# Stores of the expert blocks' result rows issued from ScalarE's queue in place of GpSimd's

## The chip, the cores and the metric

The kernel runs on one core of a Trainium2 chip. The metric is the device time of one execution in microseconds (us), from the start of the program to its end; lower is better. All values are float32.

## The reference

One inference step of a hybrid encoder layer for 336 rows (tokens) of width 1024: 64 sample rows, 16 meta rows and 256 prompt rows. Two branches (an mLSTM memory and a latent attention) are mixed and added to the rows; then every row goes to 4 of 32 experts, and a last RMSNorm follows. The change touches only the expert part:

```python
logits = x2 @ w_router + b_router
top_v, top_i = top_k(logits, 4); gates = softmax(top_v)
# rows sorted by expert, each expert's rows padded to whole blocks -> xs
def expert_block(xb, e):
    gu = xb @ w_gu[e] + b_gu[e]                    # 1024 -> 2048
    gate = minimum(gu[:, :1024], 7); up = clip(gu[:, 1024:], -7, 7)
    hid = (up + 1) * gate * sigmoid(1.702 * gate)
    return hid @ w_dn[e] + b_dn[e]                 # 1024 -> 1024
out = zeros.at[token].add(ys[dest] * gate)
```

The kernel adds the bias `b_dn` elsewhere (as gates times `b_down`), so that a block's result row is only `hid @ w_dn[e]`.

## The kernel before

Every engine has its own instruction stream, written out by hand, and the streams meet at counting semaphores. Before the expert part come the norms, the input projection, both branches and the router (to about 743 us of the span). DVE then works out, from the router's choice, how many blocks of 64 rows there are (`nb`, 39 for these inputs), which expert each block belongs to (`bei`), and which row of the sorted copy each token takes (`desti`). GpSimd (POOL) scatters the rows into a DRAM buffer `x_rows`, sorted by expert.

**The loop over blocks.** All five engines run a loop over these 39 blocks. Some experts have two blocks. An expert's weights are 12 pieces of 1 MB, each in one fixed place of the buffer `ring`: `up_w(0..7)` (gate and up weights, 8 KB in each of 128 partitions) and `dn_w(0..3)` (down weights). There is one place for each piece, so SyncE (SP) can issue the load of a piece for the next expert only when TensorE (PE) has read the piece in the current expert's last block. SP issues the loads in the order of PE's reading: `up_w(6)` and `up_w(7)` after PE's line 886, then `dn_w(0..3)` during line 906, then `up_w(0..5)` during line 878 (lines 521 and 525 are SP's).

In a block PE does, in this order: gate and up products for k = 0 to 5 (line 878), then k = 6 and 7 (line 886), transposes of the next block's rows out of `xrow` (line 546), the bias of the next block (line 867), transposes of `hid`, and the down product (line 906) into PSUM bank 4, whose halves of 64 partitions hold the two halves of the 1024 result columns. DVE clamps and multiplies (lines 1184, 1187, 1190).

ScalarE (ACT) does in each block: the sigmoid (line 1143), the copy of the turned tokens (to `xg`), the copy of the turned hidden values (`hidT`, semaphore `m_hidT`), and the copy of the result from bank 4 into `yrow`, which lies in the buffer `r_xt` (line 1149; the profile shows copies under the helper's line 933, as `r_xt<-bank`). `yrow` is a single buffer of 128 partitions by 512 columns.

POOL does in each block: the load of the next but one block's rows into `xrow` (line 1612, shown as `r_v<-x_rows`, 256 KB), the two stores of `yrow` to the DRAM buffer `y_rows` (line 1616, 64 rows of 2 KB each, 128 KB each), then it waits until the stores have landed (`m_store`) and raises `yrow_free`. PE waits for `yrow_free` before the next block's down product. After the loop POOL gathers the result rows of each token from `y_rows` (12 indirect transfers, line 1626), DVE weighs and adds them, and the last norm and the output stores follow.

In the profile's names, SPq, ACTq and POOLq are the instruction queues of those engines, and FUSED_REGOPS and MOVE there are register work for a transfer's address.

Of the kernel before, what the change touches and what calls it, by code (L numbers as in the profile page):

```python
# [33 lines left out]
NE, TOPK, BLK = 32, 4, 64  # L34
# [137 lines left out]
def build(nc, i, o, x_rows_dram, y_rows_dram):  # L172
    with ExitStack() as ctx:
# [3 lines left out]
        def sem(name):  # L177
            return ctx.enter_context(nc.semaphore(name))
# [133 lines left out]
        yrow = r_xt[:, 1280:1792]  # L312

        def up_w(k):
            at = UPSLOT[k // 2] * SLOT + 2 * D * (k % 2)
            return ring[:, at:at + 2 * D]

        def dn_w(j):
            at = DNSLOT[j // 2] * SLOT + 2 * D * (j % 2)
            return ring[:, at:at + 2 * D].rearrange("p (h f) -> p h f", h=2)  # L320
# [40 lines left out]
             "m_dve", "m_pick", "m_turn", "m_hidT", "fin_v", "fin_ss", "fin_s", "fin_out", "all_out"))  # L361
        m_rows_in, m_read = sem("m_rows_in"), sem("m_read")
        desti_set, blocks_out, x_sent = sem("desti_set"), sem("blocks_out"), sem("x_sent")
        yrow_free, zero_set, rows_zeroed = sem("yrow_free"), sem("zero_set"), sem("rows_zeroed")
        fin_y = [sem(f"fin_y{t}") for t in range(3)]
        dve_step, act_step = sem("dve_step"), sem("act_step")

# [162 lines left out]
        def _(pe):  # L530
            def begin(*name):
                n = JOB[name]
                if n >= 8:
                    pe.wait_ge(bank_free[n % 8], n // 8)
                return banks[n % 8]
# [9 lines left out]
            def turn(out, src):  # L545
                return pe.transpose(out, src, ident[0:src.shape[0], 0:src.shape[0]])  # L546
# [3 lines left out]
            b = begin("vecT")  # L550
            end(turn(b[:, 0:NVEC], vec_rows[0:NVEC, :]), "vecT")
            b = begin("convT")
            end(turn(b[:, 0:48], conv_rows[:, :]), "convT")

            for t, (c0, n) in enumerate(ROWS):
                pe.wait_ge(xn_ready, t + 1)
                for s in range(2):
                    b = begin("xT", t, s)
# [23 lines left out]
            for t in range(4):  # L582
                b = begin("cacheT", t)
# [3 lines left out]
            for name, lo, hi in (("ssq", 0, 3), ("ssk", 3, 5)):  # L587
                pe.wait_ge(cq_ready, hi)
                b = begin(name)
                end(group(b[:, 0:NT], [(cst("ones"), sq[:, k, :]) for k in range(lo, hi)]), name)  # L590
            taken(pe, "kr")
            b = begin("krs")
# [15 lines left out]
            for t, (c0, m) in enumerate(KEYS):  # L608
                b = begin("kvrow", t)
# [4 lines left out]
            b = begin("cols")  # L614
# [11 lines left out]
            for hp in range(4):  # L626
                b = begin("ukT", hp)
# [12 lines left out]
                for h in (0, 1):  # L640
                    taken(pe, "qr", hp, h)
                    b = begin("qrs", hp, h)
# [4 lines left out]
                for n in range(4):  # L647
                    h, r = n // 2, n % 2
                    b = begin("ql", hp, n)
# [56 lines left out]
                for h in (0, 1):  # L706
                    b = begin("ov", hp, h)
# [5 lines left out]
            for h in range(4):  # L713
                b = begin("wi", h)
                end(group(b[:, 0:NT], [(cst("sel", 4)[:, 128 * h:128 * h + 128], R_WI)]), "wi", h)
            for h in range(4):
                b = begin("mx", h)
                end(group(b[0:64, 0:NT], [(cst("sel", 4)[:, 128 * h:128 * h + 64], R_MX)]), "mx", h)
            pe.wait_ge(tail_done, 16)
            b = begin("convrow")  # L720
# [17 lines left out]
            for c, (c0, m) in enumerate(CHUNKS):  # L738
                q0 = qcol(c0)
                for s in range(2):  # L740
                    b = begin("krow", c, s)
# [3 lines left out]
                for s in range(2):  # L745
                    b = begin("vrow", c, s)
# [3 lines left out]
                b = begin("s", c)  # L750
# [17 lines left out]
                for h in range(4):  # L768
                    b = begin("num", c, h)
# [6 lines left out]
                for n in range(8):  # L776
                    b = begin("upd", c, n)
# [4 lines left out]
                if c in (0, 5):  # L782
                    for n in range(8):
                        taken(pe, "upd", c, n)
                    b = begin("nT", c)
# [15 lines left out]
            for t, (c0, m) in enumerate(ROWS):  # L801
                for s in range(2):
                    panel_here(pe, f"wo{s}")
                    b = begin("out", t, s)
                    end(group(b[0:m, :], [(mixed[:, k, c0:c0 + m], PV[f"wo{s}"][:, k, :]) for k in range(8)]),
                        "out", t, s)
            for t, (c0, m) in enumerate(ROWS):
                pe.wait_ge(x2_ready, t + 1)
                for s in range(2):
                    b = begin("x2T", t, s)  # L810
# [4 lines left out]
            for t, (c0, m) in enumerate(ROWS):  # L815
                for s in range(2):
                    taken(pe, "x2T", t, s)
                b = begin("lg", t)
# [3 lines left out]
            for t, (c0, m) in enumerate(ROWS):  # L822
                b = begin("pos", t)
# [3 lines left out]
            b = begin("cnt")  # L827
# [3 lines left out]
            for t, (c0, m) in enumerate(ROWS):  # L831
                pe.wait_ge(gates_set, t + 1)
                b = begin("gT", t)
                end(turn(b[0:NE, 0:m], gmat[0:m, t, :]), "gT", t)
            for t, (c0, m) in enumerate(ROWS):
                taken(pe, "gT", t)
                for s in range(2):
                    b = begin("bd", t, s)
# [5 lines left out]
            def tokens_turned():  # L844

                for k in range(8):
                    ins = turn(xt_bank[:, BLK * k:BLK * k + BLK], xrow[:, 128 * k:128 * k + 128])
                ins.then_inc(m_gath, 1)
# [7 lines left out]
            nb = pe.value_load(nbi[0:1, 0:1].bitcast(I32), min_val=NE, max_val=MAXB)  # L856
# [3 lines left out]
            def half(bank, t):  # L860
                return bank[BLK * t:BLK * t + BLK, :]

            def bias(b):

                pe.wait_ge(m_pick, b + 1)
                for q in range(4):
                    pe.matmul(half(gate_bank if q < 2 else up_bank, q % 2), pick[:, q, :], bgu[:, :],  # L867
                              start=True, stop=False, skip_group_check=True)

            bias(0)  # L870
            with pe.Fori(0, nb) as b:
                e = pe.value_load(bei[0:1, bass.ds(b, 1)].bitcast(I32), min_val=0, max_val=NE - 1)
                pe.wait_ge(m_xg, b + 1)
                for k in range(6):
                    pe.wait_ge(up_in[k], 16 * e + 16)
                    w = up_w(k)
                    for q in range(4):
                        ins = pe.matmul(half(gate_bank if q < 2 else up_bank, q % 2), xg[:, k, :],  # L878
                                        w[:, 512 * q:512 * q + 512], start=False, stop=False, skip_group_check=True)
                    ins.then_inc(m_up, 1)  # L880
                for k in (6, 7):
                    pe.wait_ge(up_in[k], 16 * e + 16)
                for bank_, q0, done in ((gate_bank, 0, m_gate), (up_bank, 2, m_up)):
                    for k in (6, 7):
                        for t in range(2):
                            ins = pe.matmul(half(bank_, t), xg[:, k, :],  # L886
                                            up_w(k)[:, 512 * (q0 + t):512 * (q0 + t) + 512], start=False,
                                            stop=(k == 7), skip_group_check=True)
                    ins.then_inc(done, 1)
                pe.wait_ge(m_xrow, 16 * b + 32)  # L890
                pe.sem_inc(m_rows_in, 1)
                tokens_turned()
                pe.wait_ge(m_read, b + 1)
                bias(b + 1)
                pe.wait_ge(m_hid, b + 1)
                for j in range(4):
                    ins = turn(ht_bank[:, 128 * j:128 * j + 128], hid[:, 128 * j:128 * j + 128])
                ins.then_inc(m_turn, 1)
                pe.wait_ge(m_hidT, b + 1)
                pe.wait_ge(yrow_free, b + 1)  # L900
                for j in range(4):
                    pe.wait_ge(dn_in[j], 16 * e + 16)
                    w = dn_w(j)
                    for h in range(2):
                        for t in range(2):
                            ins = pe.matmul(half(out_bank, t), hidT[:, j, BLK * h:BLK * h + BLK],  # L906
                                            w[:, h, 512 * t:512 * t + 512], start=(j == 0 and h == 0),
                                            stop=(j == 3 and h == 1), skip_group_check=True)
                    ins.then_inc(m_down, 1)
# [3 lines left out]
        def _(act):  # L913
# [14 lines left out]
            def signal(ins, s, v):  # L928
                ins.then_inc(s, 1)
                act.wait_ge(s, v)  # L930

            def copy(out, src, scale=1.0):
                return act.activation(out, src, ACT.Copy, scale=scale)  # L933
# [141 lines left out]
            for c, (c0, m) in enumerate(CHUNKS):  # L1075
# [7 lines left out]
                for s in range(2):  # L1083
                    filled(act, "krow", c, s)
                    p = bank(("krow", c, s))
                    h = 2 * s
# [48 lines left out]
            nb = act.value_load(nbi[0:1, 0:1].bitcast(I32), min_val=NE, max_val=MAXB)  # L1135
            def tokens():
                return copy(xg[:, :, :], banks[0][:, :].rearrange("p (k s) -> p k s", k=8))

            act.wait_ge(m_gath, 1)
            signal(tokens(), m_xg, 1)  # L1140
            with act.Fori(0, nb) as b:
                act.wait_ge(m_gt, b + 1)
                act.activation(sg, gt, ACT.Sigmoid, scale=ALPHA).then_inc(m_sig, 1)  # L1143
                act.wait_ge(m_gath, b + 2)
                tokens().then_inc(m_xg, 1)
                act.wait_ge(m_turn, b + 1)
                copy(hidT[:, :, :], banks[1][:, :].rearrange("p (j s) -> p j s", j=4)).then_inc(m_hidT, 1)
                act.wait_ge(m_down, 4 * b + 4)
                copy(yrow, banks[4][:, :]).then_inc(m_yrow, 1)
                act.wait_ge(m_yrow, b + 1)  # L1150
                act.wait_ge(moe_tab, 1)
                act.nop()


            for t, (_, n) in enumerate(ROWS):
# [392 lines left out]
        def _(pool):  # L1548
# [52 lines left out]
            pool.dma_start(xrow, x_rows_dram[0:BLK, :]).then_inc(m_xrow, 16)  # L1601
            pool.wait_ge(moe_tab, 1)
            nb = pool.value_load(nbi[0:1, 0:1].bitcast(I32), min_val=NE, max_val=MAXB)
            pool.sem_inc(yrow_free, 1)
            pool.wait_ge(m_gath, 1)
            pool.dma_start(xrow, x_rows_dram[BLK:2 * BLK, :]).then_inc(m_xrow, 16)
            with pool.Fori(0, nb) as b:
                src = x_rows_dram[bass.ds(pool.snap(b * BLK + 2 * BLK), BLK), :]
                dst = y_rows_dram[bass.ds(pool.snap(b * BLK), BLK), :]
                pool.wait_ge(m_gath, b + 2)  # L1610
                pool.wait_ge(moe_tab, 1)
                pool.dma_start(xrow, src).then_inc(m_xrow, 16)  # L1612
                pool.wait_ge(m_yrow, b + 1)
                pool.wait_ge(moe_tab, 1)
                for h in range(2):
                    pool.dma_start(dst[:, 512 * h:512 * h + 512], yrow[BLK * h:BLK * h + BLK, :]).then_inc(m_store, 16)  # L1616
                pool.wait_ge(m_store, 32 * b + 32)
                pool.sem_inc(yrow_free, 1)
            pool.wait_ge(m_store, 32 * nb)
            pool.wait_ge(m_xrow, 16 * nb + 32)  # L1620
            word = u_pad[0:1, 0, 67:68]
            pool.tensor_tensor(word, word, word, ALU.add).then_inc(blocks_out, 1)
# [50 lines left out]
```

## Time and profile before

| | |
|---|---|
| time, median of 3 runs | 1902.02 us (1899.36 to 1903.99) |
| the profiled execution | 1902.52 us |
| its span, first to last instruction | 1900.9 us |
| mean granted TensorE clock over the span | 0.948 of full |
| PE busy | 1640.6 us (86%) |
| DVE, ACT, POOL busy | 373.1, 372.1, 116.3 us |
| moved by the 16 DMA engines | 511.29 MB, mean 269 GB/s |
| expert loop | about 743 to 1854 us of the span |

"Busy" counts no register, wait or DMA-issuing work of SP and ACT. POOL's transfers do count as POOL's busy time. "To landing" is the time from the issue of a transfer to the semaphore that says its last byte is there. The span leaves out some 1.6 us of the execution's time.

### The profile page before, as it was taken

Reading aid. Unit: us, or ns where it says so; the run is one execution under the profiler, and the core shown is the slowest. Engines: PE = TensorE matmul, PEld = TensorE weight load, DVE = VectorE, ACT = ScalarE, POOL = GpSimd, SP = SyncE. Lnnn points to the kernel's source line nnn. Section 1 sums busy time; section 2 is a strip of 40 time slices with the busy share of each in tenths; the row PEclk is TensorE's granted clock in tenths of the full one; section 3 lists DMA queues with packets and bytes.
Section 4 is the critical chain, followed back from the end, with each engine's and each line's share of the span. In section 5 each row is a group of like instructions: output and inputs, shape, how many; then the busy total and the mean of one; then the engine's idle time right before and its main releaser. Section 6 shows DMA issues by size and latency. Waiting matters only on the chain.

```text
span 1900.9 us, 20283 instructions
## 1 busy us (share of the span) xinstructions
PE 1640.6 (86%) x7096; PEld 742.0 (39%) x7097; DVE 373.1 (20%) x899; ACT 372.1 (20%) x722; POOL 116.3 (6%) x220
## 2 busy tenths in 40 slices
PE   2999999999999986978788998877899978898890
PEld 1556656566666542322223332222233322232330
DVE  1444442223231134110101110101011101110114
ACT  1333432254430020111111111111111101111111
POOL 0010000000000002000000000000000000000003
PEclk9989899899999976999999999999999999999995
DMA  9355442111207425999997999999898999589884
GB/s 292 122 141 131 120 118 89 67 68 45 89 22 272 184 89 194 401 401 408 407 403 305 383 351 403 401 410 400 336 401 327 399 410 401 219 317 400 332 353 149
DMA packets 115540, 511.29 MB, mean 269 GB/s; under 512 B 11601, under 2 KB 15422, under 8 KB 82606
## 3 DMA queue, kind: packets, MB, share of 16 engines
q1 hardware_dynamic: 98862, 454.98, 61.1%
q0 software_dynamic: 16640, 55.81, 10.2%
q8 instruction: 22, 0.36, 0.1%
q14 instruction: 16, 0.13, 0.0%
HBM read 471.21 MB, written 39.55 MB: 269 GB/s over the span
## 4 chain that ended last, share of the span: by engine, by line
PE 58%; DMA 32%; DVE 4%; issue 2%; SPq 2%; ACT 1%; POOL 1%; DVEq 0%; POOLq 0%; ACTq 0%
DMA ring<-in_w_gate_up 31%; PE bank L542 31%; PE bank L878 9%; PE bank L886 8%; PE bank L906 6%; PE bank L546 2%; PE bank L867 2%; DMA ring<-in_w_in 1%; DVE r_c L1190 1%; POOL x_rows L1597 1%; DVE r_kv L1184 1%; SPq L521 1%; ACT r_kv L933 1%; SPq L433 0%; DVE r_qk L1190 0%
## 5 line engine op out<-in xcount | busy, mean ns | idle before, releaser
L878 PE MATMUL bank<-ring,r_kv 128*64 128x512 f32 x1872 | 422.4, 596 | 38.8 <-DMA ring<-in_w_gate_up 38.6
L906 PE MATMUL bank<-ring,r_kv 128*64 128x512 f32 x1248 | 276.4, 595 | 26.8 <-ACT r_kv L933 26.8
L542 PE MATMUL bank<-r_xt,ring 128*128 128x336 f32 (+2 forms) x896 | 273.7, 462 | 5.8 <-DMA ring<-in_w_in 5.4
L878 PEld LDWEIGHTS bank<-ring,r_kv 128*64 128x64 f32 x1872 | 128.5, 137 | 326.5 <-issue 226.0
L1184 DVE TENSOR_SCALAR r_kv<-bank 128x512 f32<-128x512 f32 (+1 forms) x80 | 55.0, 687 | 993.9 <-PE bank L886 981.1
L886 PE MATMUL bank<-ring,r_kv 128*64 128x512 f32 x624 | 160.3, 660 | 56.9 <-DMA ring<-in_w_gate_up 56.9
L542 PEld LDWEIGHTS bank<-r_xt,ring 128*128 128x128 f32 (+2 forms) x896 | 167.5, 190 | 98.6 <-issue 26.3
L906 PEld LDWEIGHTS bank<-ring,r_kv 128*64 128x64 f32 x1248 | 86.0, 137 | 192.1 <-issue 156.0
L1143 ACT ACTIVATE r_o<-r_kv 128x512 f32<-128x512 f32 x39 | 24.6, 630 | 544.0 <-DVE r_kv L1184 544.0
L886 PEld LDWEIGHTS bank<-ring,r_kv 128*64 128x64 f32 x624 | 51.9, 152 | 162.5 <-issue 162.5
L542 PE MATMUL bank<-ring 128*128 128x336 f32 (+4 forms) x336 | 96.4, 429 | 4.1 <-DVE ring L1343 3.9
L867 PE MATMUL bank<-bgu,r_qk 128*64 128x512 f32 x320 | 78.9, 614 | 8.8 <-DVE r_kv L1184 8.8
L933 ACT ACTIVATE r_kv<-bank 128x512 f32<-128x512 f32 (+3 forms) x85 | 49.9, 587 | 162.1 <-PE bank L546 161.8
L933 ACT ACTIVATE r_xt<-bank 128x512 f32<-128x512 f32 x39 | 23.3, 598 | 280.3 <-PE bank L906 280.3
L542 PE MATMUL bank<-ring,r_kv 128*128 128x128 f32 (+6 forms) x256 | 72.7, 421 | 2.1 <-DVE r_kv L1187 1.2
L542 PEld LDWEIGHTS bank<-ring 128*128 128x128 f32 (+4 forms) x336 | 58.1, 181 | 38.8 <-issue 15.7
L546 PEld LDWEIGHTS bank<-const,r_v 64*128 64x128 f32 (+3 forms) x524 | 45.1, 138 | 67.5 <-issue 31.9
L1616 POOL DMA_DIRECT2D y_rows<-r_xt x78 | 41.9, 537 | 414.0 <-ACT r_xt L933 411.9
L546 PE MATMUL bank<-const,r_v 64*128 64x64 f32 (+3 forms) x524 | 61.4, 253 | 1.8 <-DMA r_v<-x_rows 1.8
L542 PE MATMUL bank<-r_kv,ring 128*128 128x336 f32 (+10 forms) x240 | 60.9, 386 | 0.0
L1612 POOL DMA_DIRECT2D r_v<-x_rows x39 | 20.6, 529 | 632.9 <-PE bank L546 600.5
L542 PEld LDWEIGHTS bank<-ring,r_kv 128*128 128x128 f32 (+4 forms) x256 | 40.9, 192 | 35.7 <-issue 26.8
(213 smaller groups left out, 1001.9 us busy)
## 6 DMA issues: line engine op xcount, KB each, us to landing
ring<-in_w_gate_up SPq DMA_DIRECT2D x256, 1024.0 KB, 20.3
ring<-in_w_down SPq DMA_DIRECT2D x128, 1024.0 KB, 22.7
ring<-in_w_in SPq DMA_DIRECT2D x12, 2048.0 KB, 9.1
r_v<-x_rows POOLq DMA_DIRECT2D x41, 256.0 KB, 7.4
y_rows<-r_xt POOLq DMA_DIRECT2D x78, 128.0 KB, 5.5
x_rows<-r_c POOLq DMA_DIRECT2D x7, 1024.0 KB, 6.9
x_rows<-r_c POOLq DMA_DIRECT2D x9, 768.0 KB, 5.7
y_rows<-r_c POOLq DMA_DIRECT2D x1, 5376.0 KB, 31.1
```

What stands on the lines that cost most here:

```text
L521: sp.dma_start(up_w(k), gu[:, bass.ds(e, 1), k, :].rearrange("p a f -> p (a f)")).then_inc(up_in[k], 16)
L542: ins = pe.matmul(out, l, r, start=(n == 0), stop=(n == len(pairs) - 1), **kw)
L546: return pe.transpose(out, src, ident[0:src.shape[0], 0:src.shape[0]])
L867: pe.matmul(half(gate_bank if q < 2 else up_bank, q % 2), pick[:, q, :], bgu[:, :], start=True, stop=False, skip_group_check=True)
L878: ins = pe.matmul(half(gate_bank if q < 2 else up_bank, q % 2), xg[:, k, :], w[:, 512 * q:512 * q + 512], start=False, stop=False, skip_gr ...
L886: ins = pe.matmul(half(bank_, t), xg[:, k, :], up_w(k)[:, 512 * (q0 + t):512 * (q0 + t) + 512], start=False, stop=(k == 7), skip_group_che ...
L906: ins = pe.matmul(half(out_bank, t), hidT[:, j, BLK * h:BLK * h + BLK], w[:, h, 512 * t:512 * t + 512], start=(j == 0 and h == 0), stop=(j ...
L933: return act.activation(out, src, ACT.Copy, scale=scale)
L1143: act.activation(sg, gt, ACT.Sigmoid, scale=ALPHA).then_inc(m_sig, 1)
L1184: return dve.tensor_scalar(out, a, s1, s2, op0, op1)
L1612: pool.dma_start(xrow, src).then_inc(m_xrow, 16)
L1616: pool.dma_start(dst[:, 512 * h:512 * h + 512], yrow[BLK * h:BLK * h + BLK, :]).then_inc(m_store, 16)
```

## The change

The two stores leave POOL's loop and are issued by ACT right behind the copy that fills `yrow`. `yrow_free` goes. PE's down product now waits for the copy of the block before (`m_yrow`), which is what frees bank 4. ACT waits for the landing of the block before's stores (`m_store`) before it overwrites `yrow`. POOL keeps the loads of `xrow`, and waits for all stores once, behind its loop.

```diff
@@ PE, down product
-                pe.wait_ge(yrow_free, b + 1)
+                pe.wait_ge(m_yrow, b + 1)
@@ ACT, loop over blocks
+            act.sem_inc(m_store, 1)
+            act.sem_inc(m_yrow, 1)
             with act.Fori(0, nb) as b:
+                dst = y_rows_dram[bass.ds(act.snap(b * BLK), BLK), :]
...
                 act.wait_ge(m_down, 4 * b + 4)
+                act.wait_ge(m_store, 32 * b + 1)
                 copy(yrow, banks[4][:, :]).then_inc(m_yrow, 1)
-                act.wait_ge(m_yrow, b + 1)
+                act.wait_ge(m_yrow, b + 2)
                 act.wait_ge(moe_tab, 1)
-                act.nop()
+                for h in range(2):
+                    act.dma_start(dst[:, 512 * h:512 * h + 512], yrow[BLK * h:BLK * h + BLK, :]).then_inc(m_store, 16)
@@ POOL, loop over blocks
-            pool.sem_inc(yrow_free, 1)
...
-                dst = y_rows_dram[bass.ds(pool.snap(b * BLK), BLK), :]
                 pool.wait_ge(m_gath, b + 2)
                 pool.wait_ge(moe_tab, 1)
                 pool.dma_start(xrow, src).then_inc(m_xrow, 16)
-                pool.wait_ge(m_yrow, b + 1)
-                pool.wait_ge(moe_tab, 1)
-                for h in range(2):
-                    pool.dma_start(dst[:, 512 * h:512 * h + 512], yrow[BLK * h:BLK * h + BLK, :]).then_inc(m_store, 16)
-                pool.wait_ge(m_store, 32 * b + 32)
-                pool.sem_inc(yrow_free, 1)
-            pool.wait_ge(m_store, 32 * nb)
+            pool.wait_ge(m_store, 32 * nb + 1)
             pool.wait_ge(m_xrow, 16 * nb + 32)
```

ACT's queue before, from the table load ahead of the sigmoid to the branch back at the loop's end (`r_xt` is `yrow`'s buffer, ISA and REGISTER_ALU are register work):

```order
L1143 ACT_TABLE_LOAD
L1143 ACTIVATE r_o<-r_kv 128x512 [waits m_gt]
L1144 REGISTER_ALU
L933 ACTIVATE r_kv<-bank 128x512 [waits m_gath]
L933 ACTIVATE r_kv<-bank 128x512 [waits m_turn]
L1148 ISA
L933 ACTIVATE r_xt<-bank 128x512 [waits m_down]
L1141 REGISTER_ALU [waits moe_tab,m_yrow]
L1141 COMPARE_AND_BRANCH
```

The same place of ACT's queue in the changed kernel:

```order
L1146 ACT_TABLE_LOAD
L1146 ACTIVATE r_o<-r_kv 128x512 [waits m_gt]
L1147 REGISTER_ALU
L933 ACTIVATE r_kv<-bank 128x512 [waits m_gath]
L933 ACTIVATE r_kv<-bank 128x512 [waits m_turn]
L1151 ISA
L1152 ISA [waits m_down]
L933 ACTIVATE r_xt<-bank 128x512 [waits m_store]
L1157 ISA [waits moe_tab,m_yrow]
L1157 DMA y_rows<-r_xt 64x512
L1157 ISA
L1157 DMA y_rows<-r_xt 64x512
```

The copy now has a wait of its own for the landing of the stores before, and two DMA issues stand between it and the branch, behind which the next block's table load and sigmoid come.

POOL's queue before, from the loop's one load to the gather behind the loop:

```order
L1612 DMA r_v<-x_rows 64x1024
L1613 REGISTER_ALU
L1616 ISA [waits moe_tab,m_yrow]
L1616 DMA y_rows<-r_xt 64x512
L1616 ISA
L1616 DMA y_rows<-r_xt 64x512
L1617 ISA
L1607 REGISTER_ALU [waits m_store]
L1607 COMPARE_AND_BRANCH
L1619 REGISTER_ALU
L1620 ISA [waits m_store]
L1622 TENSOR_TENSOR u_pad<-u_pad 1x1 [waits m_xrow]
```

The same place in the changed kernel:

```order
L1615 DMA r_v<-x_rows 64x1024
L1611 REGISTER_ALU
L1611 COMPARE_AND_BRANCH
L1616 ISA
L1617 ISA [waits m_store]
L1619 ISA
L1619 TENSOR_TENSOR u_pad<-u_pad 1x1 [waits m_xrow]
```

In the last block the wait for the landing now comes behind the loop, so the loop's own closing instructions no longer follow that landing.

## Rows read from the trace of the kernel before

**Rows 1.** The page: the chain that ended last, shares of the span.

```profile
DMA ring<-in_w_gate_up 31%; PE bank L542 31%; PE bank L878 9%; PE bank L886 8%; PE bank L906 6%; PE bank L546 2%; PE bank L867 2%; DMA ring<-in_w_in 1%; DVE r_c L1190 1%; POOL x_rows L1597 1%; DVE r_kv L1184 1%; SPq L521 1%; ACT r_kv L933 1%; SPq L433 0%; DVE r_qk L1190 0%
```

**Rows 2.** Chain in order of time, expert loop: start us, us, what.

```profile
814.54 27.84 DMA ring<-in_w_gate_up
...
945.34 26.64 DMA ring<-in_w_gate_up
...
1734.94 27.85 DMA ring<-in_w_gate_up
```

**Rows 3.** DMA queues in 797 to 1004 us.

```profile
DMA packets 15410, 84.01 MB, mean 406 GB/s; under 512 B 1552, under 2 KB 1552, under 8 KB 8759
q1 hardware_dynamic: 14258, 80.60, 96.9%
```

**Rows 4.** Line 1616, the stores, over the whole execution.

```profile
L1616 POOL DMA_DIRECT2D y_rows<-r_xt x78: 529/540/544, 774.6 to 1854.8; - x78
DMA to landing us min/median/max: 2.3/5.5/6.4
```

**Rows 5.** Waits in 744 to 1900 us: waited for, us, times, longest us.

```profile
ACT r_o L1143 <- DVE r_kv L1184: 544.0, 39, 19.7
PE bank L906 <- ACT r_kv L933: 26.8, 39, 0.7
```

**Rows 6.** Timeline of ACT: a block of one expert, and the last block.

```profile
923.90 0.60 ACT L933 ACTIVATE r_xt<-bank 128x512 f32<-128x512 f32 x1 [7.19 <-PE bank L906]
924.83 1.28 ACT L1143 ACT_TABLE_LOAD   x1 [0.33 <-ACT r_xt L933]
943.70 0.63 ACT L1143 ACTIVATE r_o<-r_kv 128x512 f32<-128x512 f32 x1 [17.59 <-DVE r_kv L1184]
...
1840.74 0.63 ACT L1143 ACTIVATE r_o<-r_kv 128x512 f32<-128x512 f32 x1 [10.95 <-DVE r_kv L1184]
```

**Rows 7.** SP's issues, whole execution (ns min/median/max), and two stretches from 916 us.

```profile
L521 SPq DMA_DIRECT2D ring<-in_w_gate_up x248: 332/346/3298, 750.2 to 1817.1; - x124
L525 SPq DMA_DIRECT2D ring<-in_w_down x1: 8387/8387/8387, 924.0 to 924.0; - x1
L521 SPq DMA_DIRECT2D ring<-in_w_gate_up x1: 2823/2823/2823, 933.8 to 933.8; - x1
L521 SPq DMA_DIRECT2D ring<-in_w_gate_up x3: 877/1011/1038, 939.2 to 941.7; - x3
```

**Rows 8.** Timeline of PE, 944 to 978 us: where a block waits for its weights.

```profile
961.66 1.94 PE L878 MATMUL bank<-ring,r_kv 128*64 128x512 f32 x8 [0.70 <-DMA ring<-in_w_gate_up]
...
972.12 5.35 PE L886 MATMUL bank<-ring,r_kv 128*64 128x512 f32 x16 [3.15 <-DMA ring<-in_w_gate_up]
```

**Rows 9.** DMA queue of POOL in 924 to 934 us, one block's two stores.

```profile
q0 software_dynamic: 96, 0.26, 6.6%
```

**Rows 10.** DMA queue of SP in 365 to 373 us, one load in 2 KB rows.

```profile
q1 hardware_dynamic: 1040, 2.10, 73.5%
```

**Rows 11.** The same in 414 to 422 us.

```profile
q1 hardware_dynamic: 1024, 2.07, 68.4%
```

**Rows 12.** Chain in order of time, from the last block's copy to the gather.

```profile
1852.90 0.61 ACT r_xt L933
...
1854.76 2.49 DMA y_rows<-r_xt
...
1857.79 0.20 POOL u_pad L1622
...
1862.40 6.12 DMA ring<-y_rows,r_qk
```

**Rows 13.** Line 521, over the whole execution: the weight loads' landing.

```profile
DMA to landing us min/median/max: 4.9/20.4/28.0
```


**Rows 14.** DMA issues in 0 to 40 us: the smallest row load on SP's queue.

```profile
ring<-in_meta_tokens SPq DMA_DIRECT2D x1, 64.0 KB, 3.4
```

More of the change, by code:

```diff
@@ L363, in build @@
         desti_set, blocks_out, x_sent = sem("desti_set"), sem("blocks_out"), sem("x_sent")
-        yrow_free, zero_set, rows_zeroed = sem("yrow_free"), sem("zero_set"), sem("rows_zeroed")
+        zero_set, rows_zeroed = sem("zero_set"), sem("rows_zeroed")
         fin_y = [sem(f"fin_y{t}") for t in range(3)]
```

## The prediction

> **What bounds the kernel now.** I read the chain that ended last first, since it says which waits a saved microsecond has to lie in. Loads of the gate and up weights hold 31% of the span and PE's lines of the expert loop most of what is left there; no store and no line of ACT above 1% is in it [rows 1]. Followed in order of time, the loop falls into two kinds of blocks. In 17 of them, the first at 814.54 us and the last at 1734.94 us, the chain lies for 25 to 28 us in the landing of `up_w(7)`, issued when PE had read the one before [rows 2]. Each of these is an expert with one block behind another such expert. In the others PE itself is the limit, because an expert with two blocks gives the queue time to drain.
>
> Next the DMA queues of a stretch that holds only such single-block experts: 84.01 MB at a mean of 406 GB/s, with SP's queue alone busy for 96.9% of the 16 engines [rows 3]. So in these blocks the clock that matters is the total work of the DMA engines. An expert is 12 MB of weights, plus 0.26 MB of `xrow` and 0.26 MB of stores; one period is about 32 us (12.58 + 0.52 MB at 406 GB/s gives 32.3 us). Every microsecond of engine time that a store costs there is on the path, and everything else about the store is not.
>
> Then I look for anyone who waits for POOL's stores. PE's down product waits for `hidT` alone, 0.7 us in each of 39 blocks [rows 5]. Its wait on `yrow_free` never shows: a store lands a median 5.5 us, at most 6.4 us, after its issue [rows 4], and in the block of the rows the copy ends at 924.5 us, while the next down product comes some 24 us later. ACT is idle before each sigmoid, 544.0 us in 39 blocks, 13.9 us on average [rows 5]; in the last block, one of PE's kind, 10.95 us, in a DMA-bound one 17.59 us, both counted after the table load [rows 6].
>
> **The change, part by part.**
>
> *PE's wait for the copy in place of the landing.* The release comes some 6 us earlier, but it was early enough already. Worth 0. If the cover of some 18 us were gone, PE would gain here; no row shows such a block.
>
> *POOL loses two issues of 0.54 us [rows 4] and the wait.* What it does next in a block is the load of `xrow`, which it starts on a signal of PE that comes long after the stores have landed. Worth 0.
>
> *ACT gains two issues.* An unhindered one on SP's queue takes 0.33 to 0.35 us [rows 7]; with the address work (about 0.12 us, from SP's pace between two such issues in the chain) that is 0.47 us, so 0.94 us a block. Queued behind them are the table load (1.28 us) and the next sigmoid, for which DVE and then PE wait. They have 10.95 us of idle cover at the least that I read, so this is hidden: 0. Without cover it would be 39 x 0.94 = 37 us. The new wait for the landing of the previous stores comes 25 us or more after their issue, against 6.4 us: 0.
>
> *The store's cost to the DMA engines.* Today the two stores of a block take 6.6% of 16 engines over 10 us, 0.66 us for 0.26 MB [rows 9]. No store on a hardware queue is in the trace. The nearest thing is a load in rows of 2 KB on SP's queue: 2.10 MB in 73.5% of 8 us, 5.88 us, or 0.73 us for 0.26 MB [rows 10]; another gives 68.4% for 2.07 MB, 0.69 us [rows 11]. The difference is +0.03 to +0.07 us a block. I take +0.05, over the 17 DMA-bound blocks: +0.9 us. Bounds: from both sides it cannot cost less than nothing (-0.66 x 17 = -11 us), and if 2 KB pieces took twice the engine time that they take today, +11 us.
>
> *The tail.* Behind the last block nothing hides the store. Today the copy ends at 1853.5 us, the second store issues at 1854.76, lands 2.49 us later, and POOL's next instruction starts at 1857.79 [rows 12]. On ACT I expect the second issue at copy end + 0.1 + 0.47 + 0.12 = 1854.2. For the landing I take 2.3 us: a 1 MB load lands at best in 4.9 us [rows 13], of which 2.6 us is its transfer at 400 GB/s, leaving 2.3. That gives 1856.5 in place of 1857.25, a gain of 0.7 us. Another 0.3 us goes because the loop's closing instructions no longer stand behind that landing. The sum is -1.0 us. The bounds are the 64 KB load that took 3.4 us [rows 14], which makes it +0.1, and a landing of 2.0 us, which makes it -1.3. The gather and the additions behind it [rows 12] only move earlier.
>
> **Sum:** +0.9 - 1.0 = -0.1 us against the profiled execution's own 1902.52 us (span 1900.9 and 1.6 around it), which lies 0.5 us above the median of the three runs. About the median that is 1901.9 us; I give 1901.8. A measurement of this kernel can tell a change from none at about 0.2%, 3.8 us.
>
> **Where a rule speaks against the change.** SP's issues are not always short: one weight load held SP for 8.39 us from 924.0 us, the next for 2.82 us, and those behind it for about 1 us each, until some 942.7 us [rows 7]. ACT's copy in that block ends at 924.5 us [rows 6], so its stores would be issued in the very stretch in which SP's are held up. Nothing in the trace tells whether ACT would be held too. The Trainium skill, page Perfetto Trace Analysis, section "DMA Instruction — HWDGE (DVE, Sync)", says that the descriptor generator is shared between the two engines that issue on hardware queues and is locked for one at a time. By that rule an ACT issue would show up to some 8 us here; by the rows alone, 0.35 us. Either way the time comes out much the same, for this reason. Held until SP's 8.39 us are over, ACT has its gap from 932.4 to 933.8 us, is done near 933.5, and needs the sigmoid at 943.70 [rows 6].
>
> **The rivals.**
>
> *Slower, ACT is held past its cover.* ACT's stores wait until SP's last held issue ends, near 942.7 us. Then 0.94 us of issues and 1.28 us of table load put the sigmoid at 944.9, 1.2 us late; if each of 17 blocks grew by that, +20 us, 1922 us. Against it: PE waits for weights in the same block, 0.70 us at one place and 3.15 us at another [rows 8], and while the queue stays full a sigmoid that is 1.2 us late shifts only those waits. It decides only from about 5 us beyond the cover. This and the lock are one mechanism. Chance 3%.
>
> *Slower, the smaller pieces cost the queue more.* A store of 2 KB rows into rows 4 KB apart takes the DMA engines longer from a hardware queue, or slows SP's weights while it alternates with them. It decides above 0.22 us a block (3.8 us in 17 blocks), that is from 0.88 us for two stores. At the bound above it is +11 us, 1913 us. For it speaks that no store of this kind was seen; against it, both loads in 2 KB rows stay within 0.07 us of today's price [rows 9 to 11]. Chance 8%.
>
> *Faster, today's stores hamper the weights.* POOL's queue could be taking more from SP's than its 6.6%. Then the change gives back part of the 0.66 us a block; half of it makes -6 us, 1896 us. It decides from 0.22 us a block. Against it: in the stretch of the single-block experts the queues sum to a full 16 engines, without a gap for such a cost [rows 3]. Chance 6%.
>
> *Nothing to measure* (the forecast, with the tail anywhere in its bounds): 83%.
>
> **How the numbers follow.** Faster by over 0.2%: 0.06. Slower by over 0.2%: 0.03 + 0.08 = 0.11. Within: 0.83. The forecast's own range is the tail (-1.3 to +0.1), the DMA term (+0.5 to +1.2) and the scatter of the runs (-2.7 to +2.0), some 1898 to 1905 us. To take in the nearer part of the cases at both sides, where a cost or a gain of a few tenths of a us a block would put them, the range is 1896.5 to 1908.
>
> **What would show it.** The chain should still lie in the landing of `up_w(7)` in 17 blocks, for 25 to 28 us each, and the 406 GB/s of 797 to 1004 us should stay within 1%. Two ACT rows for the stores should appear, 78 in number, at 0.35 us where SP is not held and, if the lock holds, up to 8 us where it is. ACT's idle time before the sigmoid should fall from 13.9 to about 13 us or, with the lock, to about 10 in the mean. PE's wait for `hidT` should stay 0.7 us. From the last copy's end to POOL's next instruction should be 3.3 us in place of 4.3. The prediction is wrong if the sigmoid gets a wait on ACT's own issues, if the weight loads' landing grows by more than 0.3 us in the median, or if the DMA rate of that stretch moves by more than 1%.

## The result, and the profile after

The changed kernel takes 1906.20 us (median of 20 runs), the kernel before 1898.73 us beside it (20 runs): ratio 1.0044, 95% interval 1.0033 to 1.0054. By that ratio it is slower by 8.4 us (6.3 to 10.3); the two medians lie 7.5 us apart. The forecast was 1901.8 us and no change that can be told.

The profiled execution of the changed kernel took 1905.96 us, span 1904.3 us, 3.4 us above that of before. I read it in three stretches.

**The block loop is what it was.** The chain still lies in the landing of `up_w(7)` in 17 blocks; the first and the last of them (start us, us, what), which answer to [rows 2]:

```profile
808.52 27.79 DMA ring<-in_w_gate_up
...
1729.34 27.95 DMA ring<-in_w_gate_up
```

The DMA queues in 797 to 1004 us, to be held against [rows 3]: the same 406 GB/s, and a third queue, q10, that now carries the stores.

```profile
DMA packets 16128, 84.07 MB, mean 406 GB/s; under 512 B 1550, under 2 KB 1550, under 8 KB 9734
q1 hardware_dynamic: 14528, 80.66, 96.9%
q10 hardware_dynamic: 1120, 1.84, 2.3%
```

One block's two stores in 916 to 926 us, against 6.6% in [rows 9]: 0.69 us of the 16 engines in place of 0.66. Over all 39 blocks it is some 0.8 us a block against some 0.7 (q10 has 1.6% of the 1904 us; POOL's queue fell from 10.2% to 8.8%).

```profile
q10 hardware_dynamic: 160, 0.26, 6.9%
```

ACT's and PE's waits, as in [rows 5] (line numbers are those of the changed kernel). ACT's cover before the sigmoid fell from 13.9 to 12.7 us a block and was not used up, for all 39 sigmoids still wait for DVE; PE's wait for `hidT` is the same.

```profile
ACT r_o L1146 <- DVE r_kv L1189: 493.4, 39, 18.4
ACT L1146 <- issue: 62.1, 38, 1.8
PE bank L906 <- ACT r_kv L933: 26.8, 39, 0.7
```

**ACT's issues are not held.** All 78 of them, and then SP's down-weight issues in 915 to 930 us (ns min/median/max, first and last start):

```profile
L1157 ACTq DMA_DIRECT2D y_rows<-r_xt x78: 481/492/588, 769.1 to 1852.0; - x78
```

```profile
L525 SPq DMA_DIRECT2D ring<-in_w_down x3: 2502/4582/5948, 912.6 to 920.1; - x3
L525 SPq MOVE ring<-in_w_down x2: 29/29/29, 915.3 to 920.1; - x2
```

SP's middle issue began right behind its MOVE at 915.3 us and held SP 4.58 us, to 920 us. In that time ACT issued both stores of the block, at 916.7 and 917.4 us, in 0.48 and 0.49 us:

```profile
L1157 ACTq DMA_DIRECT2D y_rows<-r_xt x2: 481/487/493, 916.7 to 917.4; - x2
```

**The tail behind the last block is shorter, as forecast.** Chain in order of time, against [rows 12]: from the end of the last copy (1851.23 us) to POOL's next instruction it is 3.3 us in place of 4.3.

```profile
1850.62 0.61 ACT r_xt L933
...
1852.02 2.27 DMA y_rows<-r_xt
...
1854.54 0.20 POOL u_pad L1619
```

**The end is longer, and that is most of the loss.** Behind the last output store GpSimd's queue closes with a DRAIN, and the program ends only with it. First the kernel before, then the changed one; the columns are ns min/median/max and the start in us:

```profile
L173 POOLq DRAIN  x1: 1542/1542/1542, 1899.2 to 1899.2; - x1
```

```profile
L173 POOLq DRAIN  x1: 8402/8402/8402, 1895.6 to 1895.6; - x1
```

The other engines had closed theirs before (7 to 17 ns on SP, ACT and DVE, 3.2 us on PE at 1847 us). So 6.86 us stand in one instruction that no view of busy time shows and that the chain, which ends with the last store's issue, leaves out. With the tail's -0.97 us and the loop's +2.8 us that is +8.7 us; the way to the loop, shorter by 5.0 us in this execution, and 0.3 us less between the tail and the DRAIN bring it to the profiled 3.4 us. The way to the loop and most of the loop's 2.8 us are scatter, as the runs below show. DRAIN and tail alone make +5.9 us, a little less than the interval of the timed loss (6.3 to 10.3 us); what fills the rest is taken up below.

### The profile page after: what moved, and what is told of

The parts are those of the page before. It is cut to its first block, busy times and chain, and to the rows that moved or that the text cites. A ratio compares the mean times of both kernels' runs of the same rounds, so it can differ in the third digit from the quotient of the medians.

```text
span 1904.3 us, 20168 instructions
## 1 busy us (share of the span) xinstructions
PE 1636.7 (86%) x7096; PEld 738.2 (39%) x7097; DVE 372.9 (20%) x899; ACT 371.7 (20%) x722; POOL 75.3 (4%) x142
## 4 chain that ended last, share of the span: by engine, by line
PE 61%; DMA 29%; DVE 4%; issue 2%; SPq 2%; ACT 1%; POOL 1%; ACTq 0%; DVEq 0%; POOLq 0%
PE bank L542 30%; DMA ring<-in_w_gate_up 27%; PE bank L878 10%; PE bank L886 8%; PE bank L906 7%; PE bank L546 3%; PE bank L867 2%; DMA ring<-in_w_in 1%; DVE r_kv L1189 1%; DVE r_c L1195 1%; POOL x_rows L1602 1%; SPq L521 1%; ACT r_kv L933 1%; DVE r_qk L1195 0%; SPq L433 0%
```

## The experiments

I write "loop" for the time from the first bias product of PE (line 867) to the end of the last result copy: 1108.6 us before, 1111.3 us changed. "Transfers" are GpSimd's in the whole program, counted in the code: 180 before, 102 changed.

### Is the loss in the DRAIN or in the loop?

The first pair moves the four output stores to SP, which is idle at the end, in the changed kernel (e1) and in the kernel before (e2):

```diff
@@ SP, behind its weight loop
+            for t in range(3):
+                sp.wait_ge(fin_out, t + 1)
+                sp.dma_start(...).then_inc(all_out, 16)   # the stores of group t
+            sp.wait_ge(all_out, 64)
@@ POOL
-            for t in range(3):
-                pool.wait_ge(fin_out, t + 1)
...
```

> The changed kernel with its four output stores issued from SyncE's queue in place of GpSimd's, so that GpSimd's last work is the gather some 20 us before the end. Theory 1 (the lost time is mostly the wait of 8.40 us in GpSimd's closing DRAIN, 1.54 us before the change, which stands behind its last instruction): the DRAIN now runs beside the last norms, the end comes about 8 us earlier than the changed kernel's, near 1898 us, a little below or at the kernel before (1898.7). Theory 2 (the block loop itself lost the time, 8 us spread over 39 blocks by the stores on ScalarE's queue): nothing but 1 or 2 us changes, about 1905 us.

> The kernel before with the same move of its four output stores to SyncE's queue. Theory 1: only its own 1.54 us of DRAIN and some issue time are hidden, about 1896.5 us, so the changed kernel's deficit of 8.4 us shrinks to some 2 us between this and the run beside it. Theory 2: the deficit stays at 8 us.

Measured: e1 1894.08 us (12 runs), ratio to the kernel before 0.9993 (0.9981 to 1.0006). e2 1894.88 us (12 runs), 0.9986 (0.9971 to 1.0). The changed kernel's deficit of 8.4 us is down to 0.0007 x 1896 = 1.3 us, less than the intervals. GpSimd now drains beside the last norms. Its DRAIN in e1 begins at 1859.7 us, while the gathers are still being issued, and ends at 1879.3, 15 us before the end of the program (span 1894.8 us):

```profile
L173 POOLq DRAIN  x1: 19597/19597/19597, 1859.7 to 1859.7; - x1
```

Theory 1 holds and theory 2 (the loop) falls. My figures for e1 and e2 were 4 and 1.6 us too high. The kernel before took 1896.46 us beside them, 2.2 us less than the 1898.7 I reckoned from, which is all of e2's 1.6 and half of e1's 4. The move itself gave about 2 us at the end (from POOL's instruction behind the loop to the end 40.9 us in e2, 43.1 before).

### What makes the DRAIN long?

e3 uses ACT's queue once in the kernel before; e4 gives GpSimd its number of transfers back in the changed one.

```diff
@@ e3: ACT, at its start
+            act.dma_start(pad_dram[0:BLK, :], const[0:BLK, 0:8]).then_inc(m_pad, 16)
@@ e4: POOL's loop, behind the load of xrow
+                for h in range(2):
+                    pool.dma_start(pad_dram[BLK * h:BLK * h + BLK, :], const[0:BLK, 0:8]).then_inc(m_pad, 16)
+                pool.wait_ge(m_pad, 32 * b + 32)
```

> The kernel before with one small store (64 rows of 32 bytes, into a buffer of its own) issued once from ScalarE's queue near the start. If GpSimd's closing DRAIN is long because a second hardware queue is in use at all, it shows about 8.4 us and the end comes 7 us later. If it depends on what GpSimd itself issued, it stays at 1.5 us.

> The changed kernel with two small stores a block (64 rows of 32 bytes each, into a buffer of their own, waited for in the block) added to GpSimd's loop, so that GpSimd again issues as many transfers with as many rows as before the change. If the DRAIN depends on the number of transfers or descriptors that GpSimd issued, it falls back to about 1.5 us; if on the use of ScalarE's queue, it stays at about 8.4 us.

Measured: e3's DRAIN is 1542 ns (one run, 1899.0 us), e4's 1542 ns too (one run, 1901.34 us). The use of ACT's queue does not matter; what GpSimd issues does. Next its number, its size and its place:

```diff
@@ e5: no edit (the changed kernel)
@@ e6: as e4, one store a block of 64 rows
@@ e7: as e4, two stores a block of 16 rows
@@ e8: kernel before, POOL ahead of the scatter
+            for n in range(24):
+                pool.dma_start(pad_dram[0:BLK, :], const[0:BLK, 0:8]).then_inc(m_pad, 16)
+                pool.wait_ge(m_pad, 16 * n + 16)
```

> The changed kernel once more, unchanged, for a second profile. If GpSimd's closing DRAIN follows from what was issued, it is 8.40 us again to some ns; if it is chance, it moves. From the first bias product of the block loop to the last result copy the first profile has 1110.7 us against 1108.0 before; this tells how much of that is scatter.

> The changed kernel with one small store a block (64 rows of 32 bytes) in GpSimd's loop, 39 in all, half of what the run with two had. If the DRAIN falls with the number of transfers, it lies between 1.5 and 8.4 us, some 5 us. If it depends on where in a buffer that is used again and again the last one ends, it can be anything, above 8.4 too.

> The changed kernel with two small stores a block of 16 rows each in place of 64: the same number of transfers as before the change, a quarter of the rows. If the number of transfers sets the DRAIN, it is 1.5 us as with 64 rows. If the number of rows (descriptors) does, it is another value, between 1.5 and 8.4 us if it falls evenly.

> The kernel before with 24 more small stores (64 rows of 32 bytes) from GpSimd's queue before the scatter of the rows, where GpSimd is idle. If more transfers only make the DRAIN shorter, it stays at its 1.5 us. If it depends on the place in a buffer that is used again and again, it changes to another value, perhaps several us.

Measured (one run each): e5 8402 ns, to the nanosecond, at 1906.03 us, and its loop is 1107.9 us (1111.3 in the first profile of this kernel), so the loop scatters by 3 us. e6 9546 ns: more transfers, a longer DRAIN, against the even fall I had expected. e7 and e8 1542 ns, so a quarter of the rows does as well as all of them. Then all extra stores at once ahead of the scatter, where GpSimd is idle:

```diff
@@ e9, e10, e11: changed kernel, e12: kernel before; N = 78, 24, 58, 78
+            for n in range(N):
+                pool.dma_start(pad_dram[16 * n:16 * n + 16, :], const[0:16, 0:8]).then_inc(m_pad, 16)
+            pool.wait_ge(m_pad, 16 * N)
             pool.wait_ge(rows_zeroed, 16 * 17)
```

> The changed kernel with 78 small stores (16 rows of 32 bytes, rows of their own) from GpSimd's queue all at once before the scatter of the rows, where GpSimd is idle, in place of two in each block. The block loop is that of the changed kernel to the letter. If the number of GpSimd's transfers in the program sets the DRAIN, it is 1.54 us and the time falls by about 7 us, to the kernel before or 1 us below it (ratio 0.998 to 1.001). If what helps is that transfers and their waits lie between the blocks, it stays at 8.4 us or more and the ratio at 1.004.

> The same with 24 small stores: 126 transfers of GpSimd in the program in place of 102. Between 102 and 141 transfers the DRAIN grew from 8.40 to 9.55 us, 29 ns for each; by that line it is 9.1 us here.

> The same with 58 small stores: 160 transfers. By the line it would be 10.1 us; if the fall to 1.54 us comes between 141 and 160 transfers, 1.54 us or little more.

> The kernel before with 78 small stores at the same place: 258 transfers of GpSimd. If a count above some 150 ends the long DRAIN for good, it is 1.54 us. If the count starts anew at some number, it can be long again, 3 to 10 us.

Measured: e9 5707 ns, 1904.73 us (12 runs), ratio 1.0033 (1.0014 to 1.0053), so the same number of transfers as before the change, issued in a burst, takes 2.7 us off the DRAIN and mends little; e10 10362 ns (1906.94 us), e11 10526 ns (1910.09 us), e12 1542 ns (1897.38 us), one run each. The straight line through e5 and e6 failed. Four more on the cause, one of them e7's kernel, timed:

```diff
@@ e13: the same kernel as e7, timed
@@ e14: kernel before, no stores of result rows, the gather reads x_rows_dram
@@ e15: changed kernel, POOL's loop
+                pool.memset(tail[:, 0, 0, :], 0.0).then_inc(m_pad, 1)
+                pool.memset(tail[:, 1, 0, :], 0.0).then_inc(m_pad, 1)
+                pool.wait_ge(m_pad, 2 * b + 2)
@@ e16: changed kernel, behind each of the first two groups of output stores
+                for n in range(10 * g, 10 * g + 10):
+                    pool.dma_start(pad_dram[16 * n:16 * n + 16, :], const[0:16, 0:8]).then_inc(m_pad, 16)
```

> The changed kernel with two small stores a block (16 rows of 32 bytes each, waited for in the block) in GpSimd's loop, whose profile showed a DRAIN of 1.54 us, now timed against the kernel before. If the DRAIN is nearly all of the loss, the ratio falls from 1.0044 to between 0.998 and 1.001. If the stores on ScalarE's queue themselves cost time in the block loop, it stays at 1.003 or more.

> The kernel before without any stores of result rows: GpSimd's loop keeps only its load of rows, ScalarE issues nothing, and the gather reads the buffer of sorted rows instead. Left out: the experts' results do not reach the output. If GpSimd's own fewer transfers in the loop make the DRAIN long, it is 8.4 us or near it although ScalarE's queue is not used. If it takes ScalarE's stores as well, it is 1.54 us.

> The changed kernel with two small fills (128 x 3) a block in GpSimd's loop, waited for, in place of small stores. If any work on GpSimd in the loop shortens the DRAIN, it is 1.54 us; if it has to be transfers, it stays at 8 us or more.

> The changed kernel with 20 small stores (16 rows of 32 bytes) behind the first and the second group of output stores, ten each, in gaps of 8 us in which GpSimd waits for the norms. If what counts is how long ago GpSimd last issued many transfers, the DRAIN falls from 8.4 us; if unfinished work piles up with each transfer issued in a burst, as 24 and 58 early ones seemed to do, it grows to 9 us or more.

Measured: e13 1899.95 us (12 runs), ratio 1.0008 (0.999 to 1.0026): with the DRAIN at 1542 ns, 0.0036 of the 0.0044 are gone, 6.8 us (the interval of this run allows some 3 us to either side). Its closing DRAIN:

```profile
L173 POOLq DRAIN  x1: 1542/1542/1542, 1894.6 to 1894.6; - x1
```

e14, the kernel before with GpSimd's stores merely gone and ACT's queue unused, has exactly the changed kernel's DRAIN (one run, 1878.44 us). It leaves the experts' results out of the output, and its time is lower because the stores' work is left out:

```profile
L173 POOLq DRAIN  x1: 8402/8402/8402, 1868.1 to 1868.1; - x1
```

e15 8402 ns (1908.52 us), so work on GpSimd that is no transfer changes nothing. e16 (1909.56 us) has 20 transfers more and a longer DRAIN, so it is not that the last ones lie too far back:

```profile
L173 POOLq DRAIN  x1: 10036/10036/10036, 1897.6 to 1897.6; - x1
```

These figures go in steps. 8402, 10036 and 10362 ns are 1542 ns plus 84, 104 and 108 times 81.67 ns, for 102, 122 and 126 transfers: each of GpSimd's 20 or 24 more costs one step of 81.67 ns, late or early. 9546, 10526 and 5707 ns are 98, 110 and 51 steps. (The 84 stand in four runs of three different kernels, not of four as the expectation of e17 has it.) That gave a forecast for fewer transfers; e18 times e1's kernel again:

```diff
@@ e17: changed kernel, the transfers that zero x_rows
-                pool.dma_start(x_rows_dram[b0 * BLK:b1 * BLK, :] ...)     # 16 of them
+                if n % 4 == 0:                                            # 4 of them, each over four parts
+                    pool.dma_start(x_rows_dram[b0 * BLK:b1 * BLK, :] ...)
@@ e18: the same kernel as e1
```

> The changed kernel with the 16 transfers that zero the buffer of sorted rows joined into 4 of four times the size: 90 transfers of GpSimd in place of 102, the same bytes and rows. All DRAINs so far are 1.542 us plus a whole multiple of 0.0817 us: 84 times with 102 transfers in four different kernels, 104 with 20 more, 108 with 24 more. If each transfer counts once, it is 72 times here, 7.42 us. If rows or bytes count, it stays at 8.40 us.

> The changed kernel with its output stores on SyncE's queue once more, timed again beside the kernel before, to narrow the interval of the first time (0.9981 to 1.0006). With GpSimd's DRAIN covered, the shorter tail behind the last block (1.0 us) and the 1.9 us that the move itself gave at the end should put it 2 to 3 us below the kernel before, ratio 0.998 to 0.9995; if the block loop costs 2 us more with the stores on ScalarE's queue, at 1.000 or above.

Measured: e17's DRAIN is 7422 ns as forecast, 72 steps for 90 transfers, although bytes and rows are the same. Its one run took 1912.17 us: its loop begins at 750.1 us, in the other runs at 737.7 to 745.4. That the joined zeroing does this is not shown.

```profile
L173 POOLq DRAIN  x1: 7422/7422/7422, 1902.8 to 1902.8; - x1
```

e18 takes 1894.06 us (12 runs), ratio to the kernel before 0.9974 (0.9954 to 0.9994). The two timings of this kernel, 0.9993 and 0.9974, agree within their intervals. It is the changed kernel with its output stores on SP. It beats the changed kernel (1.0044) clearly. Against the kernel before it gains 0.1 and 0.3% in the two timings, and only the second interval leaves out 1. e2, the kernel before with the same move, reached 0.9986. Which of the two is better these runs don't tell.

| GpSimd's transfers | kernels | DRAIN, ns |
|---|---|---|
| 90 | e17 | 7422 |
| 102 | changed, e5, e14, e15 | 8402 |
| 122, 126 | e16, e10 | 10036, 10362 |
| 141 (39 in the loop) | e6 | 9546 |
| 160 (58 in a burst) | e11 | 10526 |
| 180 (78 in a burst) | e9 | 5707 |
| 180 (78 in the loop) | before, e3, e4, e7, e13 | 1542 |
| 204, 258 | e8, e12 | 1542 |

e1, e2 and e18 are not in the table: their DRAIN begins while the gathers still run and is longer for that.

## Why the prediction was wrong

**The step that failed** is the one on GpSimd's side: "POOL loses two issues of 0.54 us and the wait. What it does next in a block is the load of `xrow` [...] Worth 0." It followed POOL within the block, and the tail's working ended with "The gather and the additions behind it only move earlier." Neither looked at what stands behind the last store. Taking 78 transfers from GpSimd lengthened the DRAIN that closes its queue from 1.54 to 8.40 us, and nothing covers it: the program's last work, the output stores, is on that queue too. None of the rivals named it; the slower ones were on ACT and on the DMA engines. It is shown by e14 (fewer transfers alone do it), e4 and e13 (transfers given back undo it, 6.8 of 8.4 us), and e1 and e18 (covered, it costs nothing that can be told). The trace of before had the 1.54 us DRAIN but nothing that tied it to the number of transfers, so the size could not have been forecast from it. That the end of GpSimd's queue was uncovered and should have been a bound of its own, it did show. None of the signs that the prediction named for being wrong came: the sigmoid waits for DVE alone, the weight loads' median landing went from 20.4 to 20.3 us, the DMA rate stayed. All of them looked at the loop.

**The tail** was right: 3.3 us forecast, 3.31 measured. Gain 0.97 us, against 1.0 in the sum.

**The store's cost to the DMA engines** was right in size: +0.03 us in the block of the rows, at the lower bound of +0.03 to +0.07. (Over all 39 blocks it is some 0.1 us, so a store is dearer where PE sets the pace, and there the queue has room.) Whether the loop pays it cannot be told. The loops of the kernels with the stores on POOL (before, e2, e3, e8, e12) last 1105.3 to 1109.3 us, mean 1107.5; those of the changed kernel and its close relatives (changed, e1, e5, e9 to e11, e15 to e18) 1105.3 to 1111.7 us, mean 1108.5. The difference of 1.0 us fits the +0.9 forecast and is inside the scatter. With the DRAIN's +6.86 and the tail's -0.97 us it makes +6.9 us, inside the interval of the timed loss; a further 1.5 us up to its middle no run places.

The bound of -11 us, for stores that cost nothing, was not a bound. e14 has no stores, and its loop lasts 1087.3 us, 20 us less than the mean of 1107.5 (one profile), where 0.66 us in 17 blocks makes 11. So the stores cost the loop more than their share of the DMA engines in those blocks. Where the other 9 us lie is open; moving the stores to ACT's queue gave none of it back.

**ACT's cover** was right: 12.7 us left of 13.9, PE's wait for `hidT` unchanged. An issue took 0.49 us where I had 0.33 to 0.35 from SP, 0.3 us more in a block, hidden.

**The lock** of the Trainium skill (page Perfetto Trace Analysis, section "DMA Instruction — HWDGE (DVE, Sync)") did not bite: ACT issued two stores in 0.49 us each while an issue of SP stood for 4.58 us, and the longest of ACT's 78 took 0.59 us. Whatever holds SP there does not keep ACT from issuing.

**The rivals**: ACT held past its cover fell with those rows. Dearer small pieces fell at 0.69 us, under the 0.88 from which it would decide. That today's stores hamper the weights, and would do so less from ACT's queue, fell with the unchanged 406 GB/s.

**What stays open**: why the DRAIN stops growing with each transfer beyond 126, and with 180 falls to its 1.542 us when 78 of them come two a block, but only to 5.707 us when they come at once. What GpSimd does in this time no run shows.

## What to carry to other kernels

Ask of an engine that loses work what closes its queue, and whether the program's last instruction stands on it. When the last output goes through GpSimd's queue, its DRAIN is on the path, and its length depends on how many transfers GpSimd has issued and when, so a saving in the loop can come back at the end. Neither fewer nor more is simply shorter: 90 gave 7.4 us, 102 gave 8.4, 160 gave 10.5, and 180 with 78 of them in the loop 1.5. Issue the last stores from a queue whose own DRAIN is short (here SP, with 7 to 13 ns; from the tail to the end it gave 2.2 us in the kernel before and 8.6 us in the changed one), and read the last rows of every queue, not only the chain and the busy time.

## What the hardware did that I had not expected

GpSimd's closing DRAIN lasts 1.542 us plus a whole number of 81.67 ns: 72, 84, 104 and 108 of them with 90, 102, 122 and 126 transfers. It repeats to the nanosecond over kernels and chips. With 180 or more transfers, 78 of them two a block in the loop, it is down to the 1.542 us alone.

An issue on ACT's queue takes 0.48 to 0.59 us for 64 rows of 2 KB, against 0.33 to 0.38 us for SP's 1 MB loads when nothing holds them, and it goes through while an issue of SP is held for several us.
